# Issuing each Strassen product of an MLP together with its neighbour, one matmul of each in turn

## The chip, the cores and the metric

The kernel runs on 1 core of one Trainium2 chip. The metric is device time in microseconds (us) of one execution of the program. TensorE (PE) does the matmuls, and its weight loads are a row of their own (PEld); VectorE is DVE, ScalarE is ACT, GpSimd is POOL, SyncE is SP. Matmul results land in PSUM banks, all other tiles are in SBUF.

## What is computed

One layer of a hybrid encoder over 544 tokens (512 prompt, 32 sample), width 2048. The first part of the kernel (attention and mLSTM heads, output projection) is not touched. The change is in the MLP:

```python
x = x + jnp.concatenate([att, ml], axis=-1) @ p['w_out']
hn = rms_norm(x, p['norm2_w'])
x = x + jnp.square(jax.nn.relu(hn @ p['w_up'])) @ p['w_down']
```

`w_up` is 2048 x 8192 and `w_down` 8192 x 2048, all in float32. Every float32 operand is split into a high part in `fp32r` and a low part that holds the rest, and a product is the sum of three matmuls: high weights by high values, high weights by low values, low weights by high values.

## The kernel before

**Steps and products.** The MLP runs 64 steps: step 0 by 8 plain block products, steps 1 to 31 for the up projection (two tiles of 128 hidden columns each), steps 32 to 63 for the down projection. A step p from 1 on computes a 2 x 2 block result C11, C12, C21, C22 by seven products in place of eight (Strassen's scheme in Winograd's form). Product i (0 to 6) is a sum over 8 tiles k of 128, with three matmuls of 128 x 272 for each: 24 matmuls, all into one PSUM bank (`product`, L860). `Step(first, per, reg)` is a step number, inside a hardware loop one that counts with a register.

**The seven products' weights.** Each is a tile of 128 x 1024 in one of 4 slots (`SLOT`, L98): products 0 and 3 share slot 0, 1 and 4 slot 1, 2 and 6 slot 2, 5 has slot 3 alone. Weights are made in two passes. ACT copies the source to `wp_hi` (`wp_split`, L1200; I call it hi0 to hi6) when the product that used the slot before is done (`FREE_AFTER`, L100). Then DVE subtracts to get `wp_lo` (`wp_lo_part`, L1755; lo0 to lo6). The order on both is 0, 1, 5, 2, 3, 4, 6. The sources are blocks of the weight matrix loaded by SP (`wa`) or sums of them that DVE makes in `ws`: sum_1 (L1781), sum_2 (L1787), sum_3 (L1791), sum_4 (L1795). Product 3's weights come from sum_3, which stands on DVE directly behind lo2; hi3 (ACT) and lo3 (DVE) follow.

```python
SLOT = (0, 1, 2, 0, 1, 3, 2)
PLACE = (0, 1, 3, 4, 5, 2, 6)
FREE_AFTER = (-3, -2, 0, 1, 2, -1, 3)
```

**The results.** Three banks are used: y for products 0 and 4, x for 1, 3 and 5, z for 2 and 6. Products 4 and 6 accumulate on top of 0 and 2, and 3 and 5 go on top of what bank x holds. ACT copies product 0 out of its bank (`copy_y`, L1293), DVE combines the rest: `from_u` (L1872), `c22` (two instructions, L1876 and L1878), the copy of C11 (L1911 in an up step, L1998 in a down step), `c21` (L1882), `c12` (L1886).

**What follows in an up step.** DVE applies ReLU and the norm factor to C22, C21 and C12 (`relu`, L1890), ACT squares all four (L1288), and POOL makes the left-hand forms of the hidden tile with four subtractions and additions (`hidden_forms`, L567, L568, L570, L572) and stores them to memory. In a down step ACT and DVE turn a stored hidden tile into new entries of `forms_hi` and `forms_lo` (`refill`, L1348 and L1936, in three parts), and POOL adds C21/C22 and C11/C12 to the output in memory.

**Order.** Every engine works through a hand-written list, and semaphores tie the lists together: `product_done` counts finished products, `wp_hi_ready` and `wp_lo_ready` finished weights, `c11_done`, `c12_done`, `c21_done`, `c22_done`, `u_done`, `v_done` and `y_copied` results. A product waits for its own `wp_lo` and for its bank to be read. Between the up and the down steps, in step 32, the forms of the first 8 hidden tiles are loaded and converted (L430, L1277, L1767).

## Time and profile before

| | |
|---|---|
| runs | 2426.3, 2427.5, 2427.5 us; median 2427.5 |
| profiled execution | 2426.36 us, span of its records 2424.8 us |
| PE busy | 2400.3 us, 99% of the span, 18890 matmuls |
| DVE, ACT, POOL busy | 1776.0 (73%), 1084.8 (45%), 353.1 us (15%) |
| MLP steps 1 to 63 | from 1068.6 us to the last matmul's start at 2421.9 us, 10584 matmuls |
| mean granted TensorE clock | 0.998 of full speed |

The profile is one execution. A duration in it is that of one instruction from start to end; matmuls overlap, so a matmul of 0.29 us is followed by the next after some 0.126 us, and the distance of starts is what counts for PE. In the rows, "idle before" in brackets is how long the engine stood still ahead of an instruction, and what ended that.

### The profile page before, as it was taken

The page shows a single profiled execution, that of the slowest core. Times are in us where ns is not written, and L with a number is a line of the kernel's source. Part 1 is how long each engine was busy: PE and PEld are TensorE (multiplying, and loading weights), DVE is VectorE, ACT ScalarE, POOL GpSimd, SP SyncE. Part 2 cuts the span into 40 slices and gives each one's busy share as a digit, 9 for nine tenths or more (in the row PEclk, how much of TensorE's full clock was granted, in tenths as well). Part 3 has the DMA queues.
Part 4 walks back from the last instruction along what each step waited for, and adds up shares of the span by engine and source line. Part 5 has one row for each costly group of instructions (what it writes and reads, how often), then busy time and mean ns, then how long its engine had stood idle before and what let it go on. Part 6 is the DMA issues. An engine that isn't in the chain of part 4 may idle for free.

```text
span 2424.8 us, 48650 instructions
## 1 busy us (share of the span) xinstructions
PE 2400.3 (99%) x18890; PEld 2373.9 (98%) x18890; DVE 1776.0 (73%) x2568; ACT 1084.8 (45%) x1715; POOL 353.1 (15%) x408
## 2 busy tenths in 40 slices
PE   8999999999999999999999999999899999999999
PEld 8999999999999999989999999999899999999999
DVE  7466566665657664498888888888888888888887
ACT  5345353453534443364444444444544444444443
POOL 0000000000000100142222222222211101011110
PEclk9999999999999999999999999999999999999999
DMA  5423323333332524424434444444855555655554
GB/s 182 121 82 116 101 88 96 99 103 88 101 104 87 166 86 124 137 97 153 147 136 137 146 144 152 152 152 136 280 155 167 162 166 174 180 180 173 170 164 120
DMA packets 116109, 334.69 MB, mean 138 GB/s; under 512 B 13048, under 2 KB 20856, under 8 KB 116000
## 3 DMA queue, kind: packets, MB, share of 16 engines
q1 hardware_dynamic: 88352, 222.14, 28.0%
q0 software_dynamic: 26208, 106.60, 15.4%
q10 hardware_dynamic: 1440, 4.47, 0.5%
q8 instruction: 71, 1.16, 0.2%
q14 instruction: 38, 0.31, 0.0%
HBM read 274.07 MB, written 59.09 MB: 137 GB/s over the span
## 4 chain that ended last, share of the span: by engine, by line
PE 96%; DVE 2%; issue 1%; DMA 1%; ACT 0%; SPq 0%; DVEq 0%; ACTq 0%
PE psum L639 35%; PE psum L875 18%; PE psum L879 18%; PE psum L877 18%; DVE forms_lo L1767 1%; PE psum L795 1%; PE psum L664 1%; PE psum L721 1%; PE psum L735 1%; PE psum L764 1%; PE psum L679 0%; PE psum L697 0%; PE psum L695 0%; DMA form_raw<-hidden_forms 0%; PE psum L713 0%
## 5 line engine op out<-in xcount | busy, mean ns | idle before, releaser
L875 PE MATMUL psum<-forms_hi,wp_hi 128*128 128x272 f32 x3528 | 1024.6, 290 | 13.1 <-issue 8.9
L879 PE MATMUL psum<-forms_hi,wp_lo 128*128 128x272 f32 x3528 | 1022.5, 290 | 0.0
L877 PE MATMUL psum<-forms_lo,wp_hi 128*128 128x272 f32 x3528 | 1017.4, 288 | 0.0
L639 PE MATMUL psum<-act_tiles,w_hi 128*128 128x272 f32 x4544 | 758.5, 289 | 0.0
L875 PEld LDWEIGHTS psum<-forms_hi,wp_hi 128*128 128x128 f32 x3528 | 665.6, 189 | 14.6 <-issue 9.6
L877 PEld LDWEIGHTS psum<-forms_lo,wp_hi 128*128 128x128 f32 x3528 | 666.7, 189 | 0.0
L879 PEld LDWEIGHTS psum<-forms_hi,wp_lo 128*128 128x128 f32 x3528 | 665.4, 189 | 0.0
L639 PEld LDWEIGHTS psum<-act_tiles,w_hi 128*128 128x128 f32 x4544 | 642.7, 188 | 6.9 <-issue 4.0
L1200 ACT ACTIVATE wp_hi<-ws 128x1024 fp32r<-128x1024 f32 x252 | 267.3, 1061 | 625.3 <-DVE ws L1787 289.9
L639 PE MATMUL psum<-act_tiles,w_lo 128*128 128x272 f32 x2272 | 468.7, 288 | 0.0
L1755 DVE TENSOR_TENSOR wp_lo<-ws,wp_hi 128x1024 fp32r<-128x1024 f32 x252 | 309.6, 1229 | 89.0 <-ACT wp_hi L1200 87.7
L1390 DVE TENSOR_TENSOR w_lo<-w_raw,w_hi 128x512 fp32r<-128x512 f32 x288 | 200.1, 705 | 217.2 <-ACT w_hi L940 216.4
L639 PEld LDWEIGHTS psum<-act_tiles,w_lo 128*128 128x128 f32 x2272 | 355.6, 189 | 0.0
L940 ACT ACTIVATE w_hi<-w_raw 128x512 fp32r<-128x512 f32 x288 | 177.1, 627 | 318.4 <-PE psum L639 313.9
L1755 DVE TENSOR_TENSOR wp_lo<-wa,wp_hi 128x1024 fp32r<-128x1024 f32 x189 | 231.0, 1222 | 27.4 <-ACT wp_hi L1200 27.4
L1200 ACT ACTIVATE wp_hi<-wa 128x1024 fp32r<-128x1024 f32 x189 | 199.4, 1055 | 114.9 <-PE psum L879 110.6
L608 POOL DMA_DIRECT2D out_yT<-cbuf x62 | 52.2, 842 | 574.0 <-DVE cbuf L1882 499.8
L567 POOL TENSOR_TENSOR hid<-hid 128x272 f32<-128x272 f32 x32 | 37.4, 1170 | 480.7 <-ACT hid L1288 480.7
L1791 DVE TENSOR_TENSOR ws<-wa 128x1024 f32<-128x1024 f32 x63 | 94.5, 1500 | 0.0
L1781 DVE TENSOR_TENSOR ws<-wa 128x1024 f32<-128x1024 f32 x63 | 76.8, 1220 | 8.2 <-DMA wa<-in_wpairs 4.6
L1936 DVE TENSOR_TENSOR forms_lo<-hid,forms_hi 128x544 fp32r<-128x544 f32 (+1 forms) x93 | 75.7, 815 | 3.3 <-ACT forms_hi L1348 2.3
L1795 DVE TENSOR_TENSOR ws<-ws,wa 128x1024 f32<-128x1024 f32 x63 | 77.3, 1228 | 0.0
(319 smaller groups left out, 2105.8 us busy)
## 6 DMA issues: line engine op xcount, KB each, us to landing
wa<-in_wpairs SPq DMA_DIRECT2D x248, 512.0 KB, 4.4
w_raw<-in_wstream SPq DMA_DIRECT2D x291, 256.0 KB, 2.7
hidden_forms<-hid POOLq DMA_DIRECT2D x32, 952.0 KB, 4.2
hid<-hidden_forms POOLq DMA_DIRECT2D x31, 952.0 KB, 6.8
out_yT<-cbuf POOLq DMA_DIRECT2D x62, 272.0 KB, 4.6
form_raw<-hidden_forms SPq DMA_DIRECT2D x7, 1088.0 KB, 10.1
res<-in_xT POOLq DMA_DIRECT2D x16, 272.0 KB, 3.9
kc_sb<-in_kcT POOLq DMA_DIRECT2D x8, 512.0 KB, 4.3
```

Source lines behind the costliest of these rows:

```text
L639: last = nc.tensor.matmul(out[0:m, half, :], w[:, w_slot, col:col + m], x[:, half * HB:(half + 1) * HB], start=start and n_ == 0, stop=sto ...
L875: nc.tensor.matmul(bank, wp_hi[:, w, s], form_hi(i)[:, k, :], start=i < 3 and k == 0, stop=False, skip_group_check=True)
L877: nc.tensor.matmul(bank, wp_hi[:, w, s], form_lo(i)[:, k, :], start=False, stop=False, skip_group_check=True)
L879: last = nc.tensor.matmul(bank, wp_lo[:, w, s], form_hi(i)[:, k, :], start=False, stop=k == HALF - 1, skip_group_check=True)
L940: nc.scalar.activation(w_hi[:, slot, :], w_raw[:, slot, :], ACT.Copy).then_inc(hi_ready, 1)
L1200: nc.scalar.activation(wp_hi[:, SLOT[i], :], src, ACT.Copy).then_inc(wp_hi_ready, 1)
L1390: nc.vector.tensor_tensor(w_lo[:, slot, :], w_raw[:, slot, :], w_hi[:, slot, :].bitcast(f32), ALU.subtract).then_inc(lo_ready, 1)
L1755: nc.vector.tensor_tensor(wp_lo[:, SLOT[i], :], src, wp_hi[:, SLOT[i], :].bitcast(f32), ALU.subtract).then_inc(wp_lo_ready, 1)
L1781: nc.vector.tensor_tensor(ws[:, S_1, :], wa[:, A21, :], wa[:, A22, :], ALU.add).then_inc(s1_ready, 1)
L1791: nc.vector.tensor_tensor(ws[:, S_3, :], wa[:, A11, :], wa[:, A21, :], ALU.add).then_inc(s3_ready, 1)
L1795: nc.vector.tensor_tensor(ws[:, S_2, :], ws[:, S_2, :], wa[:, A12, :], ALU.add).then_inc(s4_ready, 1)
L1936: nc.vector.tensor_tensor(forms_lo[:, lo:lo + f.stop - f.start, s, :], hid[:, b, f, :], forms_hi[:, f, s, :].bitcast(f32), ALU.subtract).t ...
```

## The change

1. **Alternate issue.** A product is cut in two halves of 4 tiles k (12 matmuls). In the new `two_products` PE issues, one matmul of each in turn, the second half of product i and the first half of product i + 1 (of the next step's product 0 after product 6): 24 matmuls, which I call **phase i**. The waits of product i + 1 (`begin`) stand at the head of phase i. Steps 2 to 31 and steps 33 to 63 run so, 209 + 216 = 425 phases. The first half of each stretch's first product and the second half of its last are issued alone. Step 1 and step 32 keep whole products.
2. **Four banks.** Product 3 gets a bank of its own (bank 4), and products 3 and 5 start new sums in place of adding to bank x (`STARTS`).
3. **Output combinations.** `c22` becomes bank 4 plus `x_first`, then minus bank z; `c21` adds bank x to the first of these. The number of DVE instructions and their sizes in a steady step stay; some waits are added (`u_done`, `c22_done`).
4. **DVE order.** lo6 now stands ahead of c22, and sum_1 behind it (behind the first refill too in a down step). sum_3 and all of ACT's order, `SLOT` and `FREE_AFTER` stay.
5. **The last step** combines the old output with `x_first` and bank 4 in place of `y_first` and bank x.

```diff
+STARTS = (True, True, True, True, False, True, False)
...
-                def product(p, i, k_ready=None):
-                    bank = (bank_y, bank_x, bank_z, bank_x, bank_y, bank_x, bank_z)[i]
+                def begin(p, i):
                     pe.wait_ge(wp_lo_ready, (p * 7 + (PLACE[i] - 2)).v)
                     if i < 3:
                         pe.wait_ge((c11_done, c21_done, c12_done)[i], p.v)
                     elif i < 6:
-                        pe.wait_ge((u_done, y_copied, v_done)[i - 3], p.v)
+                        pe.wait_ge((c22_done, y_copied, u_done)[i - 3], p.v)
                     else:
                         pe.wait_ge(c22_done, (p + 1).v)
...
+                def two_products(p, i):
+                    after = (p, i + 1) if i < 6 else (p + 1, 0)
+                    begin(*after)
+                    for k in range(HALF // 2):
+                        for n_ in range(3):
+                            last = partial(i, k + HALF // 2, n_)
+                            if k == HALF // 2 - 1 and n_ == 2:
+                                last.then_inc(product_done, 1)
+                            partial(after[1], k, n_)
...
+                product(Step(2), 0, ks=early)
+                with pe.Fori(0, PAIRS - 3) as r:
                     for i in range(7):
-                        product(Step(2, 1, r), i)
+                        two_products(Step(2, 1, r), i)
+                for i in range(6):
+                    two_products(Step(PAIRS - 1), i)
+                product(Step(PAIRS - 1), 6, ks=late)
...
                 def c22(p):
+                    dve.wait_ge(u_done, p.v)
                     dve.wait_ge(product_done, (p * 7 + 4).v)
-                    nc.vector.tensor_tensor(cbuf[:, 1, 1, :], bank_x, y_first[:], ALU.subtract).then_inc(v_done, 1)
+                    nc.vector.tensor_tensor(cbuf[:, 1, 0, :], bank_4, x_first[:], ALU.add).then_inc(v_done, 1)
                     dve.wait_ge(v_done, p.v)
-                    nc.vector.tensor_tensor(cbuf[:, 1, 1, :], cbuf[:, 1, 1, :], bank_z, ALU.subtract).then_inc(c22_done, 1)
+                    nc.vector.tensor_tensor(cbuf[:, 1, 1, :], cbuf[:, 1, 0, :], bank_z, ALU.subtract).then_inc(c22_done, 1)
...
                     sum_4(p)
...
-                    sum_1(p + 1)
+                    wp_lo_part(p, 6)
                     dve.wait_ge(squared, (p * 4).v)
                     c22(p)
                     relu(p, cbuf[:, 1, 1, :], 1, c22_done)
-                    wp_lo_part(p, 6)
+                    sum_1(p + 1)
```

PE in the loop over the up steps, where product 3 begins. In a MATMUL row the tile that PE writes stands first, then the two it reads; a row's brackets hold what it waits for. Before, product 3's first matmul stands behind the whole of product 2:

```order
L879 MATMUL psum<-forms_hi,wp_lo 128x272
L864 REGISTER_ALU
L875 MATMUL psum<-forms_hi,wp_hi 128x272 [waits u_done,wp_lo_ready]
L877 MATMUL psum<-forms_lo,wp_hi 128x272
L879 MATMUL psum<-forms_hi,wp_lo 128x272
L875 MATMUL psum<-forms_hi,wp_hi 128x272
```

And with the change; the row with the wait is product 2's fifth tile (phase 2), and product 3's first matmul is the one behind it:

```order
L878 MATMUL psum<-forms_hi,wp_lo 128x272 x2
L864 REGISTER_ALU
L878 MATMUL psum<-forms_hi,wp_hi 128x272 [waits c22_done,wp_lo_ready]
L878 MATMUL psum<-forms_hi,wp_hi 128x272
L878 MATMUL psum<-forms_lo,wp_hi 128x272 x2
L878 MATMUL psum<-forms_hi,wp_lo 128x272 x2
```

The wait for product 3's weights now stands 12 matmuls earlier, and holds the second half of product 2 too.

DVE in the same loop, from product 6's end on, with the change (L1913 is c12, L1917 a ReLU, L1780 `wp_lo_part`: here lo2, then lo3 behind sum_3, L1816, then lo4 and lo6; L1897 is `from_u`, L1820 sum_4):

```order
L1913 TENSOR_TENSOR cbuf<-psum,x_first 128x272 [waits product_done]
L1917 SCALAR_TENSOR_TENSOR cbuf<-cbuf,rstd 128x272 [waits c12_done]
L1777 REGISTER_ALU
L1780 TENSOR_TENSOR wp_lo<-ws,wp_hi 128x1024 [waits wp_hi_ready]
L1816 TENSOR_TENSOR ws<-wa 128x1024 [waits wp_lo_ready]
L1777 REGISTER_ALU
L1780 TENSOR_TENSOR wp_lo<-ws,wp_hi 128x1024 [waits wp_hi_ready]
L1897 TENSOR_TENSOR x_first<-psum,y_first 128x272 [waits y_copied,product_done,c12_done]
L1777 REGISTER_ALU
L1780 TENSOR_TENSOR wp_lo<-wa,wp_hi 128x1024 [waits wp_hi_ready]
L1820 TENSOR_TENSOR ws<-ws,wa 128x1024 [waits wp_lo_ready]
L1777 REGISTER_ALU
```

And before, the same stretch (L1886 is c12, L1890 a ReLU, L1755 `wp_lo_part`, L1791 sum_3, L1872 `from_u`, L1795 sum_4):

```order
L1886 TENSOR_TENSOR cbuf<-psum,x_first 128x272 [waits product_done]
L1890 SCALAR_TENSOR_TENSOR cbuf<-cbuf,rstd 128x272 [waits c12_done]
L1752 REGISTER_ALU
L1755 TENSOR_TENSOR wp_lo<-ws,wp_hi 128x1024 [waits wp_hi_ready]
L1791 TENSOR_TENSOR ws<-wa 128x1024 [waits wp_lo_ready]
L1752 REGISTER_ALU
L1755 TENSOR_TENSOR wp_lo<-ws,wp_hi 128x1024 [waits wp_hi_ready]
L1872 TENSOR_TENSOR x_first<-psum,y_first 128x272 [waits y_copied,product_done,c12_done]
```

Nothing has moved between c12 and sum_4; the swap of lo6, c22 and sum_1 comes behind it.

## Rows read from the trace of the kernel before

**Rows 1.** The page: busy time of the engines.

```profile
PE 2400.3 (99%) x18890; PEld 2373.9 (98%) x18890; DVE 1776.0 (73%) x2568; ACT 1084.8 (45%) x1715; POOL 353.1 (15%) x408
```

**Rows 2.** What PE waited for from 1069 us on (total us, times, longest).

```profile
PE psum L875 <- issue: 8.9, 4, 5.0
PE psum L875 <- DVE wp_lo L1755: 4.3, 3, 2.2
```

**Rows 3.** L875 alone, 1500.2 to 1700: count, durations, first and last start.

```profile
L875 PE MATMUL psum<-forms_hi,wp_hi x528: 287/290/292, 1500.2 to 1699.6; 128*128 128x272 f32 x176
```

**Rows 4.** L639 alone, 938.4 to 1040.85, the output projection: same columns.

```profile
L639 PE MATMUL psum<-act_tiles,w_hi x544: 283/288/293, 938.4 to 1040.4; 128*128 128x272 f32 x182
L639 PE MATMUL psum<-act_tiles,w_lo x272: 282/288/291, 938.9 to 1040.7; 128*128 128x272 f32 x136
```

**Rows 5.** PE in step 0, two plain products by turns into two banks.

```profile
1057.32 0.41 PE L894 MATMUL psum<-forms_hi,wp_hi 128*128 128x272 f32 x2
...
1060.33 0.41 PE L894 MATMUL psum<-forms_hi,wp_hi 128*128 128x272 f32 x2
```

**Rows 6.** PE: last matmul of step 15's product 6, first of step 16's product 0.

```profile
1390.40 0.29 PE L879 MATMUL psum<-forms_hi,wp_lo 128*128 128x272 f32 x1
1390.53 0.29 PE L875 MATMUL psum<-forms_hi,wp_hi 128*128 128x272 f32 x1
```

**Rows 7.** ACT in up step 16: hi2, hi3.

```profile
1390.73 1.06 ACT L1200 ACTIVATE wp_hi<-ws 128x1024 fp32r<-128x1024 f32 x1 [0.58 <-PE psum L879]
...
1394.87 1.06 ACT L1200 ACTIVATE wp_hi<-ws 128x1024 fp32r<-128x1024 f32 x1 [2.44 <-DVE ws L1791]
```

**Rows 8.** DVE in up step 16: lo2, sum_3, lo3.

```profile
1391.82 1.22 DVE L1755 TENSOR_TENSOR wp_lo<-ws,wp_hi 128x1024 fp32r<-128x1024 f32 x1
1392.96 1.79 DVE L1791 TENSOR_TENSOR ws<-wa 128x1024 f32<-128x1024 f32 x1
1395.96 1.25 DVE L1755 TENSOR_TENSOR wp_lo<-ws,wp_hi 128x1024 fp32r<-128x1024 f32 x1 [1.21 <-ACT wp_hi L1200]
```

**Rows 9.** POOL in up steps 16 and 17: the first operation on each hidden tile.

```profile
1392.51 1.16 POOL L567 TENSOR_TENSOR hid<-hid 128x272 f32<-128x272 f32 x1 [14.59 <-ACT hid L1288]
...
1413.70 1.16 POOL L567 TENSOR_TENSOR hid<-hid 128x272 f32<-128x272 f32 x1 [14.62 <-ACT hid L1288]
```

**Rows 10.** DVE by groups: sum_3 in up steps (1100:1700), in down steps (1800:2370).

```profile
L1791 DVE TENSOR_TENSOR ws<-wa 128x1024 f32<-128x1024 f32 x28 | 50.1, 1790 | 0.0
L1791 DVE TENSOR_TENSOR ws<-wa 128x1024 f32<-128x1024 f32 x27 | 32.9, 1219 | 0.0
```

**Rows 11.** ACT, then DVE in down step 45: hi2; c12, lo2, sum_3, lo3.

```profile
2019.63 1.06 ACT L1200 ACTIVATE wp_hi<-ws 128x1024 fp32r<-128x1024 f32 x1 [0.68 <-PE psum L879]
...
2020.40 0.43 DVE L1886 TENSOR_TENSOR cbuf<-psum,x_first 128x272 f32<-128x272 f32 x1
2020.75 1.22 DVE L1755 TENSOR_TENSOR wp_lo<-ws,wp_hi 128x1024 fp32r<-128x1024 f32 x1
2021.89 1.22 DVE L1791 TENSOR_TENSOR ws<-wa 128x1024 f32<-128x1024 f32 x1
2024.31 1.23 DVE L1755 TENSOR_TENSOR wp_lo<-ws,wp_hi 128x1024 fp32r<-128x1024 f32 x1 [1.21 <-ACT wp_hi L1200]
```

**Rows 12.** DVE and PE where PE waited for weights, in step 1.

```profile
1071.01 1.22 DVE L1755 TENSOR_TENSOR wp_lo<-ws,wp_hi 128x1024 fp32r<-128x1024 f32 x1
...
1072.28 0.39 PE L875 MATMUL psum<-forms_hi,wp_hi 128*128 128x272 f32 x1 [0.47 <-DVE wp_lo L1755]
1072.51 0.29 PE L877 MATMUL psum<-forms_lo,wp_hi 128*128 128x272 f32 x1
```

**Rows 13.** Stretches: span, busy PE PEld DVE ACT POOL, granted clock, DMA share, GB/s.

```profile
1390.53:1411.72 21.19, 21.19 (x171) 21.19 (x170) 17.20 (x21) 8.88 (x12) 5.83 (x5) 1.00 0.43 145
1729.51:1765.19 35.68, 25.83 (x170) 25.01 (x169) 34.63 (x35) 22.64 (x28) 8.85 (x8) 0.86 0.79 274
2019.43:2040.62 21.19, 21.19 (x171) 21.19 (x169) 17.50 (x21) 9.48 (x11) 2.24 (x3) 1.00 0.58 172
```

More of the change, by code:

```diff
@@ L203, in build @@
         bank_y, bank_x, bank_z, bank_4 = (psum[:, i, 0:HB] for i in range(4))
+        BANKS = (bank_y, bank_x, bank_z, bank_4, bank_y, bank_x, bank_z)
         b11, b12, b21, b22 = (res[:, k, t] for k in (slice(HALF, KT), slice(0, HALF))
@@ L866, in product, with partial @@
                     elif i < 6:
-                        pe.wait_ge((u_done, y_copied, v_done)[i - 3], p.v)
+                        pe.wait_ge((c22_done, y_copied, u_done)[i - 3], p.v)
                     else:
                         pe.wait_ge(c22_done, (p + 1).v)
-                    for k in range(HALF):
+                    if p.first >= PAIRS + 1 and i in (0, 3, 5):
+                        pe.wait_ge(refill_lo, ((p + (-PAIRS)) * 3 + {0: -2, 3: -1, 5: 0}[i]).v)
+                def partial(i, k, n_):
+                    s, w = slice(k * P, (k + 1) * P), SLOT[i]
+                    weights, form = ((wp_hi, form_hi(i)), (wp_hi, form_lo(i)), (wp_lo, form_hi(i)))[n_]
+                    return nc.tensor.matmul(BANKS[i], weights[:, w, s], form[:, k, :], start=STARTS[i] and k == 0 and n_ == 0,
+                                            stop=k == HALF - 1 and n_ == 2, skip_group_check=True)
@@ L871, in product @@
+                def product(p, i, k_ready=None, ks=range(HALF)):
+                    if ks[0] == 0:
+                        begin(p, i)
+                    for k in ks:
                         if k_ready is not None and k % 4 == 0:
                             pe.wait_ge(form_lo_ready, k_ready + 1 + k // 4)
-                        s = slice(k * P, (k + 1) * P)
-                        w = SLOT[i]
-                        nc.tensor.matmul(bank, wp_hi[:, w, s], form_hi(i)[:, k, :], start=i < 3 and k == 0, stop=False,
-                                         skip_group_check=True)
@@ L877, in product @@
-                        nc.tensor.matmul(bank, wp_hi[:, w, s], form_lo(i)[:, k, :], start=False, stop=False,
-                                         skip_group_check=True)
-                        last = nc.tensor.matmul(bank, wp_lo[:, w, s], form_hi(i)[:, k, :], start=False,
-                                                stop=k == HALF - 1, skip_group_check=True)
-                    last.then_inc(product_done, 1)
+                        for n_ in range(3):
+                            last = partial(i, k, n_)
@@ new lines, in product @@
+                    if ks[-1] == HALF - 1:
+                        last.then_inc(product_done, 1)
[3 more added lines that the diff above has]
+                    for k in range(HALF // 2):
+                        for n_ in range(3):
+                            last = partial(i, k + HALF // 2, n_)
+                            if k == HALF // 2 - 1 and n_ == 2:
+                                last.then_inc(product_done, 1)
+                            partial(after[1], k, n_)
@@ L914, in _ @@
                     product(Step(1), i, 2 * FORM_AT[i])
+                early, late = range(HALF // 2), range(HALF // 2, HALF)
+                product(Step(2), 0, ks=early)
+                with pe.Fori(0, PAIRS - 3) as r:
+                    for i in range(7):
+                        two_products(Step(2, 1, r), i)
+                for i in range(6):
+                    two_products(Step(PAIRS - 1), i)
+                product(Step(PAIRS - 1), 6, ks=late)
+                for i in range(7):
+                    product(Step(PAIRS), i, 2 * (FORMS_UP + i))
+                product(Step(PAIRS + 1), 0, ks=early)
                 with pe.Fori(0, PAIRS - 2) as r:
                     for i in range(7):
[L917 to L928 removed]
+                        two_products(Step(PAIRS + 1, 1, r), i)
+                for i in range(6):
+                    two_products(Step(2 * PAIRS - 1), i)
+                product(Step(2 * PAIRS - 1), 6, ks=late)
             @block.scalar
@@ L1291, in copy_y @@
                     act.wait_ge(product_done, (p * 7 + 1).v)
-                    act.wait_ge(c21_done, p.v)
+                    if not (p.reg is None and p.first == 1):
+                        act.wait_ge(u_done, (p + (-1)).v)
                     nc.scalar.activation(y_first[:], bank_y, ACT.Copy).then_inc(y_copied, 1)
@@ L1986, in down @@
                         refill(t + (-1), 2)
-                    sum_1(p + 1)
-                    refill(t, 0)
+                    wp_lo_part(p, 6)
                     if first:
@@ L1993, in down @@
                     c22(p)
-                    wp_lo_part(p, 6)
+                    refill(t, 0)
+                    sum_1(p + 1)
                     if not first:
```

20 lines of the change are left out of this document (7 added, 13 removed).

## Prediction

> **What bounds the kernel now.** I read the page's busy times first: PE is busy 99% of the span [rows 1], so only two things can move the time: the distance between the starts of matmuls, and waits of PE that do not exist now. The list of PE's waits says how few there are: from the MLP's start at 1069 us on, 13.2 us in 7 waits [rows 2], all in steps 1 and 32. The stretches show it too: up step 16 and down step 45 last 21.19 us each, and PE is busy for all of it [rows 13].
>
> Next the distance of starts. A product is all in one bank. L875 is one matmul in three, and its 528 in steps 21 to 30 start from 1500.2 to 1699.6 [rows 3]: 199.4 us / (527 x 3) = **126.1 ns**. At the granted clock of 1.00 [rows 13], 2.4 GHz, 272 columns are 113 ns of streaming, so 13 ns are something else. The output projection has matmuls of the same size and writes two banks by turns. Its 816 run from 938.4 to 1040.7 [rows 4]: 102.3 / 815 = **125.5 ns**. In step 0 two products with different weights go by turns into two banks, and 24 matmuls take 1060.33 - 1057.32 = 3.01 us [rows 5], 125.4 ns.
>
> Last, the chain that makes weights, since every phase asks for its weights earlier. In step 16 product 6's last matmul of the step before starts at 1390.40 [rows 6]. hi2, which needs its slot, starts at 1390.73, then hi3 at 1394.87 [rows 7]; on DVE lo2, sum_3 and lo3 run from 1391.82, 1392.96 and 1395.96, the last until 1397.21 [rows 8]. Each waits for the one before: product 6, hi2 (ACT), lo2 (DVE), sum_3 (DVE), hi3 (ACT), lo3 (DVE). From hi2's start to lo3's end it is **6.48 us** in an up step. In down step 45 it is 2024.31 + 1.23 - 2019.63 = **5.91 us** [rows 11].
>
> **Part 1, the matmuls' distance.** The 425 phases hold 10,200 matmuls. They write two banks by turns, as in [rows 4, 5], and with different weights in turn, as in [rows 5]. I take 125.4 ns: 0.7 ns x 10,200 = **-7.1 us**. Bounds: nothing, if the 0.7 ns come from what else differs in those rows; 1.0 ns, if the rounded starts of [rows 5] hide 0.3, so -10.2 us.
>
> The Trainium skill (TensorE: Matmul & The Clock Gate, Back-to-back issue gap) gives N / 2.4 + 2.5 ns as the distance of warm matmuls, for 272 columns an estimate of 116 ns. No row here shows it, in one bank or in two; if alternating reached it, this term would be -105 us, taken alone.
>
> **Part 2, the wait for product 3's weights.** This decides. Before, product 0 frees slot 0 at its end, and product 3 starts two products later. Now product 3 starts at the head of phase 2, which is two phases behind product 6's end: 48 x 125.4 = 6.02 us after the end of phase 6. lo3 must be done by then, and its chain starts only with product 6's end. It used to have three products for it, 9.08 us.
>
> Up step: product 6's last matmul is now the last but one of its phase, so the phase ends 2 x 0.125 us after its start, and hi2 starts 0.33 - 0.25 = 0.08 us behind the phase's end (0.33 is 1390.73 - 1390.40, [rows 6, 7]). The chain adds 6.48: 6.56. Where PE waited for weights in step 1, the matmul started 0.05 us after lo's end at 1072.23, and the next followed after 0.23 instead of 0.126 us [rows 12]: 0.15 us more, 6.71. PE is ready at 6.02, so it stands **0.70 us**. This falls in steps 2 to 31, 30 times (in step 2 half a product more lies ahead of phase 2, but the chain is late there from step 1 as well): **+21.0 us**.
>
> Down step: 0.08 + 5.91 + 0.15 = 6.14, which is 0.12 us too late. Here lo2 starts at 2020.75, on the heels of c12 (2020.40), though hi2 was done at 2020.69 [rows 11]. DVE's own queue is as late as ACT, and PE's faster phases bring the demand some 0.03 us nearer; PE also has register instructions between its waits for the refill and the weights. I take **0.20 us**, 30 times (steps 34 to 63; step 33 has the half product ahead): **+6.0 us**. Bounds 0.05 and 0.35: +1.5 and +10.5 us.
>
> The up step's size hangs on sum_3. It takes 1.79 us in up steps and 1.22 in down steps [rows 10], and in up steps POOL's L567 runs from 1392.51 to 1393.67 across its start at 1392.96 [rows 8, 9]. POOL starts when the last square is made, which hangs on c12 and hi2, so on product 6's end as sum_3 does. Both keep their distance, and the 0.57 us stay. Bounds: 0 and 1.16 us (L567's whole length) in place of 0.57, which is 0.13 to 1.29 us of wait, +4 to +39 us; I stay at the row, since nothing moves one against the other.
>
> The Trainium skill (SBUF — State Buffer, Who interferes with whom) has DVE instructions with two SBUF inputs and POOL instructions that read SBUF lock each other out for a whole instruction. sum_3 would then wait for L567's end, 1393.67 - 1392.96 = 0.71 us, where the row shows 0.57; the sum with 0.71 is 4 us higher.
>
> **Part 3, the other waits, at nothing.** Product 4 needs lo4 one phase after product 1's end. hi and lo together last 2.34 us (hi3's start to lo3's end, [rows 7, 8]); with 0.08 and 0.15 that is 2.6 of 3.01 us. Product 2 needs lo2 one phase after product 6: 1391.82 + 1.22 - 1390.73 = 2.31, the same. Product 6 waits for c22: two DVE instructions behind product 3's end, within one phase, as lo6 now stands ahead and is made a phase earlier. If this cover went, each of them would cost what it is late by, 61 times. sum_1 moved back by some 3 us, and its wait and the loads of `wa` it reads have only more time; the copy of C11 behind it still waits for product 4's end. ACT's copy of bank y lies between hi3 and hi4 as before. DVE's busy time in a step stays 17.2 and 17.5 of 21.19 us [rows 13].
>
> **Part 4, the ends of the stretches.** Step 32 lasts 35.68 us with a granted clock of 0.86 [rows 13], because forms are loaded and converted; those loads wait for step 31's products. Each of these now ends half a product later against PE's total work, 1.5 us, and the last phases of step 31 bring PE there 0.7 us later by its own wait: **+0.8 us**. Bounds -1 and +6: a longer standstill can hold the clock at its lower level, 1.2 GHz, for longer. The end of the kernel hangs on product 6 of step 63 as before: nothing.
>
> **Sum.** -7.1 + 21.0 + 6.0 + 0.8 = +20.7 us on the profiled execution's 2426.4 us: **2447 us**. That execution lies 1.1 us below the median of the runs, less than I can resolve. A measurement of this kernel tells 0.2%, 4.9 us, from no change. A steady up step would last 6.02 + 0.70 + 5 x 3.01 = 21.8 us, a down step 21.3.
>
> **Rivals.**
>
> *Alternating gives nothing.* The distance stays at 126.1 ns. Then +7.1 is missing from the gain, less some 2 us, as phases 0 and 1 are longer by 0.03 us in all and the wait shorter by as much: 2452 us. For it: [rows 4] have other operands, too. Against it: [rows 5] have the MLP's own. 17%.
>
> *sum_3 is not slowed.* If POOL's work and sum_3 move apart, the up steps wait 0.13 us: 2447 - 17 = 2430 us, no change that can be told. Against it stands what I said of their common start. 8%.
>
> *The weights are in time.* The other side: the chain fits into two phases, PE never waits, and the gain of the first part is left: 2426.4 - 7.1 + 0.8 = 2420 us, faster. The place is the head of phase 2, and it decides at 6.02 - 0.15 - 0.08 = 5.79 us from hi2's start to lo3's end. The rows have 5.91 and 6.48, so DVE and ACT would have to be quicker by 0.1 and 0.7 us with unchanged instructions. 4%.
>
> *Matmuls much closer.* If writing one bank all the time is what costs most of the 13 ns, phases could shrink to 24 x 116 = 2.78 us. DVE's chain from product 4's end on then sets the step: in a down step 12.2 us to product 3's start (4 phases, 12.04 us, are what it has at 125.4 ns, with 0.2 over) and three phases, 20.6 us, in an up step 21.0. Against 21.19 that is -18 and -6 us: 2404 us. 116 ns is the figure of the page named above; from rows alone, -20.7 us is made good at 2.7 ns less on the 120 matmuls outside phases 0 and 1, 122.7 ns. Nothing in [rows 4, 5] is below 125.4. 4%.
>
> *The clock falls.* If a standstill of 0.7 us in every up step let the clock drop to 1.2 GHz for a time, a phase at that level would take 3.01 us more. For it: step 32's 0.86. Against it: there PE stood 9.9 us of 35.68 (busy 25.83, [rows 13]), and in steps of 21 us it would stand 3% of the time. Were it one phase in every second up step: 2447 + 15 x 3.01 = 2492 us. 3%.
>
> **How the numbers follow.** Forecast 62%, the rivals 17, 8, 4, 4 and 3%; 2% for something slower that I don't see. Faster by over 0.2%: the two rivals and a sliver, 9%. Within 0.2%: the unslowed sum_3, 8%. Slower: the rest, 83%. The range reaches from above the unslowed sum_3, 2433 (half the up steps' wait gone and 10.2 us gained), to 2460: no gain by alternating, 0.35 us in down steps and a worse step 32 (2452 + 4 + 4). Below it lie 13%, above it some 5%.
>
> **What would show it.** In the profile of the changed kernel: starts of matmuls inside a phase 125.4 ns apart; PE's waits led by `wp_lo`, some 60 times, at the head of phase 2 and nowhere else, about 0.6 us in up and 0.1 in down steps; step lengths of 21.8 and 21.3 us; sum_3 still 1.79 us in up steps. I am wrong if PE waits elsewhere, above all for lo2 or lo4; if sum_3 is back at 1.22 us there; or if the mean clock is below 0.99.

## The result and the profile after

The changed kernel takes **2449.1 us** (median of 4 runs, 2447.5 to 2449.9), the kernel before 2427.5 us (2426.3 to 2428.4). The ratio is 1.0088, with a 95% interval of 1.0071 to 1.0106: 21.6 us slower. The profiled execution has a span of 2447.4 us against 2424.8 us, 22.6 us more. The forecast was 2447 us, so the total is right; not all of its terms are.

The page of the changed kernel, busy times [rows 1]:

```profile
PE 2409.3 (98%) x18890; PEld 2370.3 (97%) x18890; DVE 1781.6 (73%) x2569; ACT 1084.7 (44%) x1715; POOL 353.7 (14%) x408
```

What PE waited for from 1069 us on, in total us, times and longest [rows 2]:

```profile
PE psum L878 <- DVE wp_lo L1780: 26.1, 38, 3.7
PE psum L878 <- DVE forms_lo L1792: 0.3, 1, 0.3
```

The same work (18890 matmuls), and 13 us of recorded waits have become 26 us, now nearly all for `wp_lo` (L1780 here). Short gaps are missing in this list: it counts 38 waits, while the starts of matmuls show 58 gaps at the head of phase 2 alone. So the distances of starts are what to read. Step 16, PE, the end of phase 6 with the first matmul of the step's phase 0 (x2: two matmuls in one row), then the last row of phase 1 and the head of phase 2:

```profile
1400.75 0.41 PE L878 MATMUL psum<-forms_hi,wp_lo 128*128 128x272 f32 x2
1401.00 0.42 PE L878 MATMUL psum<-forms_hi,wp_hi 128*128 128x272 f32 x2
...
1406.75 0.41 PE L878 MATMUL psum<-forms_hi,wp_lo 128*128 128x272 f32 x2
1407.63 0.52 PE L878 MATMUL psum<-forms_hi,wp_hi 128*128 128x272 f32 x2 [0.47 <-DVE wp_lo L1780]
1407.99 0.41 PE L878 MATMUL psum<-forms_lo,wp_hi 128*128 128x272 f32 x2
```

ACT, DVE and POOL in the same step: hi2, lo2, sum_3, hi3, lo3, and POOL's four operations on the hidden tile (L569 to L574) [rows 7 to 9]:

```profile
1401.08 1.06 ACT L1224 ACTIVATE wp_hi<-ws 128x1024 fp32r<-128x1024 f32 x1 [0.53 <-PE psum L878]
...
1402.17 1.23 DVE L1780 TENSOR_TENSOR wp_lo<-ws,wp_hi 128x1024 fp32r<-128x1024 f32 x1
1402.86 1.18 POOL L569 TENSOR_TENSOR hid<-hid 128x272 f32<-128x272 f32 x1 [15.14 <-ACT hid L1312]
1403.32 1.80 DVE L1816 TENSOR_TENSOR ws<-wa 128x1024 f32<-128x1024 f32 x1
...
1404.00 1.75 POOL L570 TENSOR_TENSOR hid<-hid 128x272 f32<-128x272 f32 x1
...
1405.23 1.06 ACT L1224 ACTIVATE wp_hi<-ws 128x1024 fp32r<-128x1024 f32 x1 [2.45 <-DVE ws L1816]
...
1405.71 0.79 POOL L572 TENSOR_TENSOR hid<-hid 128x272 f32<-128x272 f32 x1
...
1406.33 1.25 DVE L1780 TENSOR_TENSOR wp_lo<-ws,wp_hi 128x1024 fp32r<-128x1024 f32 x1 [1.21 <-ACT wp_hi L1224]
...
1406.58 1.64 POOL L574 TENSOR_TENSOR hid<-hid 128x272 f32<-128x272 f32 x1
```

The chain is the one of before, instruction for instruction. From hi2's start to lo3's end it takes 1407.58 - 1401.08 = 6.50 us (6.48 before). Phase 2, which holds product 3's first half, starts at 1407.63, 0.05 us behind lo3's end. The last matmul of phase 1 starts at 1406.88, so the gap is 0.75 us in place of 0.125, and the next distance 0.23 in place of 0.125: 0.63 + 0.10 = 0.73 us are lost. This stands in each of steps 3 to 31 (step 31 loses 0.05 us more), and nowhere else in them.

Step 45, a down step [rows 11]: hi2, c12 (L1913), lo2, sum_3, hi3, lo3, and ahead of c12 the conversion of the refill (L1963):

```profile
2042.50 1.06 ACT L1224 ACTIVATE wp_hi<-ws 128x1024 fp32r<-128x1024 f32 x1 [0.62 <-PE psum L878]
...
2042.69 0.72 DVE L1963 TENSOR_TENSOR forms_lo<-hid,forms_hi 128x544 fp32r<-128x544 f32 x1
...
2043.33 0.43 DVE L1913 TENSOR_TENSOR cbuf<-psum,x_first 128x272 f32<-128x272 f32 x1
...
2043.68 1.22 DVE L1780 TENSOR_TENSOR wp_lo<-ws,wp_hi 128x1024 fp32r<-128x1024 f32 x1
...
2044.81 1.22 DVE L1816 TENSOR_TENSOR ws<-wa 128x1024 f32<-128x1024 f32 x1
...
2046.14 1.06 ACT L1224 ACTIVATE wp_hi<-ws 128x1024 fp32r<-128x1024 f32 x1 [2.58 <-DVE ws L1816]
...
2047.23 1.23 DVE L1780 TENSOR_TENSOR wp_lo<-ws,wp_hi 128x1024 fp32r<-128x1024 f32 x1 [1.20 <-ACT wp_hi L1224]
```

lo3 is done at 2048.46, 5.96 us after hi2's start, and phase 2 starts at 2048.60: gap 0.30 us, with the slow next distance 0.28 us lost. Sixteen down steps look so. Twelve others lose 0.18 to 0.2 us, and one (step 38) loses 0.46. Step 63 has no gap and only the slow next distance, 0.10 us.

The stretches of step 16, of step 45 and of step 32 [rows 13]. Columns: span, busy PE, PEld, DVE, ACT, POOL, granted clock, DMA share, GB/s:

```profile
1748.91:1782.21 33.30, 26.32 (x168) 25.32 (x168) 33.20 (x33) 20.54 (x25) 7.96 (x7) 0.85 0.84 288
1401.00:1422.76 21.76, 21.29 (x170) 21.07 (x169) 17.32 (x21) 8.87 (x12) 5.84 (x5) 1.00 0.40 141
2042.42:2063.72 21.30, 21.28 (x170) 21.07 (x169) 17.52 (x21) 9.48 (x11) 2.23 (x3) 1.00 0.56 171
```

An up step lasts 21.76 us and a down step 21.30, in place of 21.19.

A place that the forecast left out is where alternation starts. PE in step 2: the last matmul of product 0's first half, which is issued alone, then phase 0:

```profile
1093.54 0.29 PE L878 MATMUL psum<-forms_hi,wp_lo 128*128 128x272 f32 x1
1095.62 0.51 PE L878 MATMUL psum<-forms_hi,wp_hi 128*128 128x272 f32 x2 [1.80 <-DVE wp_lo L1780]
```

PE stands 2 us for product 1's weights. DVE makes C11's copy, lo0, sum_2, and only then can hi1 and lo1 follow. Step 33 has the same gap (1783.70 to 1785.78). And behind both gaps the granted clock falls, 1.5 us after the gap's end in step 2 and 0.8 us in step 33. Two stretches of one length in step 2:

```profile
1095.62:1100.52 4.90, 4.89 (x27) 4.90 (x28) 4.64 (x5) 2.01 (x5) 2.44 (x2) 0.65 0.34 107
1100.52:1105.42 4.90, 4.90 (x41) 4.90 (x41) 2.67 (x3) 2.29 (x3) 3.36 (x4) 1.00 0.72 265
```

27 matmuls in 4.90 us and then 41. Some 15 of them are 0.227 us apart, at the lower level of 1.2 GHz: 1.5 us lost, twice.

**The account**, from the starts of the MLP's 10584 matmuls, after minus before, in us:

| place | us | forecast |
|---|---|---|
| 10,200 matmuls at 125.09 in place of 126.11 ns | -10.4 | -7.1 |
| head of phase 2, steps 3 to 31 (29 x 0.73) | +21.3 | +21.0 |
| head of phase 2, steps 34 to 62 (29 gaps, 7.1) and step 63 (0.1) | +7.2 | +6.0 |
| ahead of step 1, and step 1 itself (0.7 - 2.5) | -1.8 | 0 |
| start of alternation, steps 2 and 33 (2.0 + 2.1) | +4.1 | 0 |
| clock at 1.2 GHz behind these (2 x 1.5) | +3.0 | 0 |
| ahead of step 32 and step 32 itself (1.4 - 2.4) | -1.0 | +0.8 |
| sum | +22.4 | +20.7 |

The starts themselves end 22.6 us apart; 0.2 us stay unplaced.

### The profile page after: what moved, and what is told of

It is laid out like the page before. It is cut to its first block, busy times and chain, and to the rows that moved or that the text cites. A ratio compares the mean times of both kernels' runs of the same rounds, so it can differ in the third digit from the quotient of the medians.

```text
span 2447.4 us, 48692 instructions
## 1 busy us (share of the span) xinstructions
PE 2409.3 (98%) x18890; PEld 2370.3 (97%) x18890; DVE 1781.6 (73%) x2569; ACT 1084.7 (44%) x1715; POOL 353.7 (14%) x408
## 4 chain that ended last, share of the span: by engine, by line
PE 86%; DVE 8%; ACT 3%; issue 2%; DMA 1%; DVEq 0%; ACTq 0%; SPq 0%
PE psum L878 45%; PE psum L641 34%; ACT wp_hi L1224 3%; DVE wp_lo L1780 2%; DVE ws L1816 2%; DVE forms_lo L1792 1%; PE psum L797 1%; PE psum L666 1%; PE psum L723 1%; PE psum L737 1%; PE psum L766 1%; DMA form_raw<-hidden_forms 0%; PE psum L681 0%; PE psum L699 0%; PE psum L697 0%
## 5 line engine op out<-in xcount | busy, mean ns | idle before, releaser
L878 PE MATMUL psum<-forms_hi,wp_hi 128*128 128x272 f32 x3528 | 747.4, 290 | 26.7 <-DVE wp_lo L1780 26.1
L878 PE MATMUL psum<-forms_hi,wp_lo 128*128 128x272 f32 x3528 | 742.6, 289 | 0.0
L878 PE MATMUL psum<-forms_lo,wp_hi 128*128 128x272 f32 x3528 | 741.0, 288 | 0.0
L878 PEld LDWEIGHTS psum<-forms_hi,wp_hi 128*128 128x128 f32 x3528 | 559.3, 189 | 40.5 <-DVE wp_lo L1780 30.0
L878 PEld LDWEIGHTS psum<-forms_lo,wp_hi 128*128 128x128 f32 x3528 | 563.6, 189 | 0.0
L878 PEld LDWEIGHTS psum<-forms_hi,wp_lo 128*128 128x128 f32 x3528 | 557.8, 189 | 0.0
L1780 DVE TENSOR_TENSOR wp_lo<-ws,wp_hi 128x1024 fp32r<-128x1024 f32 x252 | 310.2, 1231 | 144.9 <-ACT wp_hi L1224 144.8
L1224 ACT ACTIVATE wp_hi<-wa 128x1024 fp32r<-128x1024 f32 x189 | 199.5, 1055 | 134.1 <-PE psum L878 129.6
L1780 DVE TENSOR_TENSOR wp_lo<-wa,wp_hi 128x1024 fp32r<-128x1024 f32 x189 | 230.7, 1221 | 27.0 <-ACT wp_hi L1224 27.0
L569 POOL TENSOR_TENSOR hid<-hid 128x272 f32<-128x272 f32 x32 | 37.8, 1182 | 499.8 <-ACT hid L1312 499.8
L1816 DVE TENSOR_TENSOR ws<-wa 128x1024 f32<-128x1024 f32 x63 | 94.9, 1506 | 0.0
L1820 DVE TENSOR_TENSOR ws<-ws,wa 128x1024 f32<-128x1024 f32 x63 | 77.4, 1228 | 0.0
L1812 DVE TENSOR_TENSOR ws<-wa,ws 128x1024 f32<-128x1024 f32 x63 | 76.8, 1220 | 0.0
```

What stands on the lines that cost most here:

```text
L569: nc.gpsimd.tensor_tensor(h[:, 2, :], h[:, 0, :], h[:, 7, :], ALU.subtract).then_inc(term_ready, 1)
L878: return nc.tensor.matmul(BANKS[i], weights[:, w, s], form[:, k, :], start=STARTS[i] and k == 0 and n_ == 0, stop=k == HALF - 1 and n_ == ...
L1224: nc.scalar.activation(wp_hi[:, SLOT[i], :], src, ACT.Copy).then_inc(wp_hi_ready, 1)
L1780: nc.vector.tensor_tensor(wp_lo[:, SLOT[i], :], src, wp_hi[:, SLOT[i], :].bitcast(f32), ALU.subtract).then_inc(wp_lo_ready, 1)
L1812: nc.vector.tensor_tensor(ws[:, S_2, :], wa[:, A11, :], ws[:, S_1, :], ALU.add).then_inc(s2_ready, 1)
L1816: nc.vector.tensor_tensor(ws[:, S_3, :], wa[:, A11, :], wa[:, A21, :], ALU.add).then_inc(s3_ready, 1)
```

## The experiments

Twelve kernels, in three batches. In their diffs "-" is the kernel that each starts from. For the distance of matmuls I give the mean of all starts inside products or phases (about 10,000 in each kernel, without gaps over 0.14 us), and where it decides the row of a group of matmuls from 1500 to 1700 us, from which it can be had to 0.1 ns as in [rows 3].

### Is it sum_3 on the chain? sum3_early and pool_after_sum3

sum3_early, from the changed kernel: sum_3 is made a product earlier, directly behind sum_2, and what stood ahead of lo2 and can wait goes behind it. The diff is of an up step; in a down step sum_3 moves likewise, and `refill(t, 1)` goes behind lo2.

```diff
+                    sum_3(p + 1)
...
-                    relu(p, cbuf[:, 1, 0, :], 0, c21_done)
...
-                    relu(p, cbuf[:, 0, 1, :], 1, c12_done)
                     wp_lo_part(p + 1, 2)
-                    sum_3(p + 1)
+                    relu(p, cbuf[:, 1, 0, :], 0, c21_done)
...
+                    relu(p, cbuf[:, 0, 1, :], 1, c12_done)
```

> The changed kernel with sum_3 of the next step taken on DVE directly behind sum_2 instead of behind lo2; the ReLU of C21 moves behind c12, in down steps the second refill behind lo2, so that lo2 keeps its place. My theory: PE's waits at the head of phase 2 come from the chain product 6, hi2, lo2, sum_3, hi3, lo3. With sum_3 out of it, hi3 needs only product 0's end, and lo3 is done some 0.5 us before PE asks. All waits of 0.63 us (up) and 0.2 us (down) go, the distance of matmuls stays at 125.1 ns: about 2449 - 22 - 8 = 2419 us, faster than before by 0.3%. Rival: two phases are too short for ACT and DVE in any order, and the wait only moves, to lo2 at phase 1 or to c22 at phase 5: 2435 us or more, with waits at another product. PE's list of waits tells them apart.

Measured: **2420.4 us** (2419.8 to 2421.0), ratio 0.9972 (0.9962 to 0.9983). Its up steps last 21.03 to 21.08 us, its down steps 21.00. PE's waits from 1069 us on:

```profile
PE psum L878 <- DVE wp_lo L1780: 12.3, 8, 2.3
PE psum L878 <- DVE forms_lo L1792: 0.3, 1, 0.3
```

DVE by groups, 1100 to 1700 (us in total, mean ns; L1816 is sum_3, L1780 the `wp_lo` made from `ws`):

```profile
L1780 DVE TENSOR_TENSOR wp_lo<-ws,wp_hi 128x1024 fp32r<-128x1024 f32 x114 | 151.8, 1332 | 78.7 <-ACT wp_hi L1224 78.7
L1816 DVE TENSOR_TENSOR ws<-wa 128x1024 f32<-128x1024 f32 x28 | 34.2, 1220 | 0.0
```

The steady waits are gone, but for 0.05 us in an up step (in the changed kernel L1780 means 1233 and L1816 1801 ns there). POOL now meets lo3, which takes 1.61 us in step 16 and is still done 0.12 us before phase 2 starts. The gaps of steps 2 and 33 stay, at 2.35 us. So the order of a few DVE instructions decides the sign of this change.

pool_after_sum3 keeps the changed kernel's DVE order, and holds POOL back instead:

```diff
+                    pool.wait_ge(s3_ready, (p + 1).v)
                     nc.gpsimd.tensor_tensor(...)
```

> The changed kernel with POOL's work on a hidden tile waiting for sum_3 as well. My theory: 0.57 us of the up steps' wait is sum_3 being slowed by POOL's subtraction across its start. sum_3 then takes 1.22 us in up steps, PE's wait there falls from 0.63 to about 0.1 us: 2449 - 17 = 2432 us; down steps stay. Rival: POOL's work now meets lo3 instead, which becomes longer by about as much: sum_3 at 1.22, lo3 at 1.8 us, time within 5 us of 2449. Second rival: POOL has nothing to do with it, sum_3 stays at 1.79.

Measured: **2436.7 us** (2436.3 to 2437.5), ratio 1.0040 (1.0025 to 1.0055). Between the two. DVE and POOL in step 16: sum_3, lo3 (L1781 here), and POOL's two operations beside it:

```profile
1397.95 1.22 DVE L1817 TENSOR_TENSOR ws<-wa 128x1024 f32<-128x1024 f32 x1
1399.26 0.77 POOL L570 TENSOR_TENSOR hid<-hid 128x272 f32<-128x272 f32 x1 [16.09 <-DVE ws L1817]
...
1399.99 0.77 POOL L571 TENSOR_TENSOR hid<-hid 128x272 f32<-128x272 f32 x1
...
1400.38 1.46 DVE L1781 TENSOR_TENSOR wp_lo<-ws,wp_hi 128x1024 fp32r<-128x1024 f32 x1 [1.21 <-ACT wp_hi L1225]
...
1400.72 1.76 POOL L573 TENSOR_TENSOR hid<-hid 128x272 f32<-128x272 f32 x1
```

sum_3 is back at 1.22 us, so POOL was what stretched it: shown. But the next link, lo3, takes 1.46 us in place of 1.25, since POOL now meets that one. Of the 21 us lost at the head of phase 2 in the up steps 11 are left, where my expectation, 17 us off the total, would have left 4. Its first rival, POOL meeting lo3, came true in part: the collision moved along the chain instead of leaving it.

The rows of both kernels say how much such a meeting costs. In the table, the overlap is the time from an instruction's start to the end of the other engine's instruction that was under way; unhindered, the DVE instructions take 1.22 us and POOL's 0.77.

| instruction, and what was under way at its start | overlap, us | longer by |
|---|---|---|
| sum_3 behind POOL's L569 | 0.72 | 0.58 |
| POOL's L569 behind lo2 | 0.54 | 0.41 |
| POOL's L570 behind sum_3 | 1.12 | 0.98 |
| POOL's L574 behind lo3 | 1.00 | 0.87 |
| lo3 behind POOL's L572 | 0.17 | 0.03 |
| pool_after_sum3: lo3 behind POOL's L571 | 0.38 | 0.24 |
| pool_after_sum3: POOL's L573 behind lo3 | 1.12 | 0.99 |

Each is longer by its overlap less 0.13 or 0.14 us: whichever started second waited for the end of the first. The steps from 1120 to 1700 us show the same throughout.

### What do the other parts do? whole_products

From the changed kernel: four banks, regrouped combinations and DVE order stay, and each product is issued whole.

```diff
-                        two_products(Step(2, 1, r), i)
+                        product(Step(2, 1, r), i)
```

> The changed kernel with whole products issued one after another as before; four banks, the new output combinations and the new order on DVE stay. My theory: these parts cost and bring nothing; the distance of matmuls is 126.1 ns, PE has no waits in steady steps (two whole products lie between product 6 and product 3), 21.19 us a step: 2427.5 us, within 3 us. Rival: the output combinations or the order bring or cost something of their own, then it differs by more than that.

Measured: 2424.4 us (2423.7 to 2425.5), ratio 0.9990 (0.9981 to 1.0000): just under the kernel before, by less than 0.2%. I had expected 2427.5 within 3 us, so it lies at that edge. The distance is 126.11 ns and no steady step waits. Its 2 us against before lie at the ends of the stretches: step 1 gains 2.5 us and step 2 gives 1.7 back, step 32 gains 2.6 and step 33 gives 1.1 back. Which of the three parts gives these 2 us was not tested. As they cost nothing together, the loss of the changed kernel is all in the alternate issue.

### What brings the matmuls closer? Eight kernels

My forecast put the smaller distance down to two banks used by turns. **two_banks_before**, from the kernel before, sends every second matmul to bank 7, which nobody reads, so half of each sum is left out:

```diff
+                            odd = (3 * k + n_ + 1) % 2
-                        nc.tensor.matmul(bank, ...)
+                            last = nc.tensor.matmul(psum[:, 7, 0:HB] if odd else bank, ...)
```

> The kernel before, whole products one after another, but in steps 1 to 63 every second matmul writes another bank that nobody reads, so half of each product's sum is left out. Tells whether the bank or the mixing of products brings matmuls closer. If the bank does it, as I hold: the distance falls from 126.1 to 125.1 ns, a steady step lasts 168 x 125.1 = 21.02 us, and the kernel about 2427 - 10 = 2417 us. If it is that weights and values of two products come by turns: 126.1 ns and 2427 us.

Measured: 2426.5 us in its one run, so the expectation missed. Its matmuls of one kind, 1500 to 1700 us:

```profile
L877 PE MATMUL psum<-forms_hi,wp_lo x530: 287/289/291, 1499.8 to 1699.9; 128*128 128x272 f32 x177
```

200.1 us / (529 x 3) = 126.1 ns, as before. **one_bank_alternating** is the counterpart, from the changed kernel; only a product's last matmul goes to its own bank, and the sums are left out of the output:

```diff
-                    return nc.tensor.matmul(BANKS[i], ...)
+                    end = k == HALF - 1 and n_ == 2
+                    return nc.tensor.matmul(BANKS[i] if end else psum[:, 7, 0:HB], ...)
```

> The changed kernel with its alternating order, waits and semaphores, but all matmuls of an MLP product except the last of each write bank 7; only a product's last goes to its own bank (so the sums are left out of the output). Theory A, mixing: the smaller distance of starts inside a phase comes from the weights and values of two products in turn, not from two banks. Then the distance stays at 125.1 ns and the time near 2449 us. Theory B, banks (my prediction's): in one bank the distance is back at 126.1 ns, and the time is 2449 + 10.5, less some 2 us of shorter standstills, near 2457 us. I expect A, 125.1 ns.

Measured: 2449.1 us in its one run, 125.08 ns inside phases, and 21.3 us lost at the head of phase 2 in the up steps, as in the changed kernel. Both agree: **the bank has no part in it**. What is left is the order in which the matmuls read their operands.

The next idea: weights or values that follow each other twice cost 3.3 ns. **k_pairs_before**, from the kernel before, puts another tile's matmul between:

```diff
-                    for k in range(HALF):
+                    order = [(k + h, n_) for k in range(HALF // 2) for n_ in range(3) for h in (0, HALF // 2)]
+                    for j, (k, n_) in enumerate(order):
```

> The kernel before, whole products as they are, but within a product tiles k and k + 4 are issued one matmul of each in turn (the product with the stepwise wait in the first steps keeps its order). Same bank, no wait moved. Theory A, in its simplest form: what costs the 1 ns is that the same weights, or the same values, follow each other back to back; with another tile's between them the distance falls to 125.1 ns, and the time by 10.3 us to about 2417 us, 0.9957 of the kernel before. Rival: two different products are needed (their tiles lie in different slots), then 126.1 ns and 2427 us, ratio 1.000. I expect 2417 us, with little certainty.

Measured: **2416.6 us** (2415.2 to 2417.1), ratio 0.9956 (0.9943 to 0.9970). Here two of six matmuls are of this kind, first of a pair to second of a pair:

```profile
L879 PE MATMUL psum<-forms_lo,wp_hi x534: 284/287/291, 1499.8 to 1699.4; 128*128 128x272 f32 x178
```

From the first of a pair to the second of the last pair: 199.6 us / (266 x 6 + 1) = **125.0 ns**. The whole gain of alternating is there inside one product, with no weights wanted earlier. The expected time was met by luck: it came from the idea of repeats, which the next kernels refute.

The remaining kernels change the same line only; `order` lists the pairs of tile k and matmul (0 high by high, 1 high by low, 2 low by high):

```diff
+order = [(k, n_) for k in range(HALF) for n_ in (0, 2, 1)]                                     # values_twice_before
+order = [(k, n_) for k in range(HALF) for n_ in (2, 0, 1)]                                     # two_repeats_before
+order = [(k + h, n_) for k in range(0, HALF, 2) for n_ in range(3) for h in (0, 1)]            # neighbour_tiles_before
+order = [(k + h, n_) for k in range(HALF // 2) for h in (0, HALF // 2) for n_ in range(3)]     # tile_jumps_before
```

no_repeats_before issues matmul 0 of each tile one tile later: 1 and 2 of tile k, then 0 of tile k - 1.

> The kernel before, with the three matmuls of a tile in the order high weights by high values, low weights by high values, high weights by low values: now the values repeat back to back, and the weights do not. If the 1 ns comes from weights that repeat (one repeat in three before, none here), the distance falls to 125.1 ns, about 2417 us. If it comes from values that repeat (none inside a tile before, one here), it rises, to some 127 ns, about 2437 us. If repeats do not matter, it stays at 126.1 ns and 2427 us. I expect the first.

Measured: 2427.4 us in its one run, 126.11 ns. My expectation missed; the repeats had only changed from weights to values, so the idea could still stand. The last batch was to count repeats.

> The kernel before, with each tile's order low weights by high values, high by high, high by low: two of three matmuls repeat something of the one ahead (first the values, then the weights). Theory A, repeats at 3.3 ns each: 125.00 + 2 x 1.11 = 127.2 ns, 10,500 matmuls by 1.1 ns more, about 2439 us, 1.0047. Theory C, distance of tiles: the order of tiles is unchanged, so 126.1 ns and 2427 us. I expect A.

Measured: 2427.4 us (2426.5 to 2428.1), ratio 1.0002 (0.9992 to 1.0011), 126.11 ns. Missed.

> The kernel before, one product at a time, tiles in order, but each tile's high-by-high matmul is issued one tile later (high by low and low by high of tile k, then high by high of tile k - 1). No matmul shares weights or values with the one ahead of it. Theory A, repeats: a matmul that has its weights or its values in common with the one ahead costs 3.3 ns (the 1.11 ns by which 126.11 exceeds 125.00, on one of three matmuls). Then 125.0 ns and about 2416 us, 0.9957. Theory C, tiles: what counts is how far apart in SBUF the tiles of neighbours lie (4 tiles in the kernel that pairs k and k + 4), not repeats; then it stays near 126.1 ns, 2427 us. I expect A.

Measured: 2421.5 us (2421.0 to 2422.6), ratio 0.9978 (0.9969 to 0.9988), 125.56 ns: neither theory's number. One in three of its matmuls:

```profile
L879 PE MATMUL psum<-forms_hi,wp_hi x532: 285/288/289, 1499.8 to 1699.8; 128*128 128x272 f32 x178
```

> The kernel before, with tiles k and k + 1 (k even) issued one matmul of each in turn: no repeat, and the tiles lie next to each other in SBUF. Theory A, repeats: 125.0 ns, about 2416 us. Theory C, distance of tiles: near 126.1 ns, about 2427 us. I expect A.

Measured: 2419.1 us in its one run, 125.28 ns; missed by little, but the difference is real in the records (pairs again, 200.1 / 1597 = 125.3):

```profile
L879 PE MATMUL psum<-forms_hi,wp_hi x534: 286/288/290, 1499.8 to 1699.9; 128*128 128x272 f32 x178
```

> The kernel before, with whole tiles (three matmuls each, one repeat in three as before) in the order 0, 4, 1, 5, 2, 6, 3, 7. Theory A, repeats: 126.1 ns and 2427 us. Theory C, distance of tiles: the distance falls for the matmul at each change of tile, between 125.0 and 125.8 ns, 2416 to 2424 us. I expect A.

Measured: **2416.4 us** in its one run, 125.00 ns (199.9 us / (533 x 3) = 125.0):

```profile
L879 PE MATMUL psum<-forms_lo,wp_hi x534: 287/288/296, 1499.8 to 1699.7; 128*128 128x272 f32 x178
```

I had expected 2427 us. This fells the theory of repeats: whole tiles, one repeat in three as before, and the full gain. Together, by what a product's 24 matmuls take over 24 x 125.00 ns:

| order of tiles | repeats in 3 | ns | over, per product |
|---|---|---|---|
| 0 1 2 ... (before, two_banks, values_twice) | 1 | 126.11 | 26.7 |
| 0 1 2 ..., two_repeats | 2 | 126.11 | 26.7 |
| 1 1 0 2 2 1 ..., no_repeats | 0 | 125.56 | 13.3 |
| 0 1 0 1 0 1 2 3 ..., neighbour_tiles | 0 | 125.28 | 6.7 |
| 0 4 0 4 0 4 1 5 ..., k_pairs | 0 | 125.00 | 0 |
| 0 0 0 4 4 4 1 1 1 ..., tile_jumps | 1 | 125.00 | 0 |

What counts is **the order in which a product's tiles are read**. Orders that take tiles 4 apart together have no surplus; the plain order has 26.7 ns a product, 3.3 ns for each of its 8 tiles. The changed kernel pairs tile k + 4 of one product with tile k of the next, which is 4 apart too, and this fits its 125.09 ns.

Why the order counts is not settled. A tile is 512 bytes of weights and 1088 bytes of values in a partition, so its addresses are one suspect, but no run moved the tiles themselves. And the surplus can't be put down to single changes of tile. Over 53 steady steps the mean distance ahead of each of a product's first six matmuls is 122.5, 120.9, 134.1, 125.0, 121.7 and 124.2 ns in k_pairs_before, and the same to 0.1 ns in tile_jumps_before and in phase 0 of the changed kernel, although the first changes tile at every matmul and the second at every third. In the kernel before it is 126.7, 127.5, 127.5, 126.7, 130.0 and 120.0 ns, and the same in values_twice_before. Only the sum over a product is shown to follow the order.

### The version that comes out: k_pairs_regrouped

whole_products with k_pairs' order inside each product:

```diff
+                        for k in range(HALF // 2):
+                            for n_ in range(3):
+                                partial(i, k, n_)
+                                last = partial(i, k + HALF // 2, n_)
```

> The changed kernel's four banks, output combinations and DVE order with whole products (which took 2424.4 us, distance 126.1 ns), and within each product tiles k and k + 4 one matmul of each in turn. If repeats of the same weights or values are the cause of the 1 ns: 2424.4 - 10.3 = 2414 us, 0.9948 of the kernel before, with no steady wait for product 3's weights. If two different products are needed: 2424 us, ratio 0.999.

Measured: **2413.3 us** (2412.6 to 2413.5), ratio 0.9943 (0.9930 to 0.9957), the fastest of all. The expected 2414 us was taken from the idea of repeats, so here too the number was right and its reason wrong. PE's waits from 1069 us on, and a stretch that lasts as long as one up step:

```profile
PE psum L878 <- DVE wp_lo L1775: 9.4, 8, 2.2
PE psum L878 <- DVE forms_lo L1787: 0.3, 1, 0.3
```

```profile
1400.00:1421.00 21.00, 21.00 (x171) 21.00 (x170) 17.31 (x21) 8.87 (x13) 5.82 (x5) 1.00 0.43 147
```

Steps of 21.00 us, with PE busy throughout.

## Why the prediction was right, and where not

**What bounds the kernel, and the failing link: right.** The wait named (product 3's weights, at the head of phase 2), its chain and its size held: 0.73 us against 0.70 in up steps, with a chain of 6.50 us against 6.48. It falls 29 times, not 30. sum3_early takes one link out and with it the loss.

**sum_3 and POOL: right.** They kept their distance (1404.04 - 1403.32 = 0.72 us of overlap, 1.80 us for sum_3), so the 0.57 us stayed. pool_after_sum3 and sum3_early both bring 1.22 us back. That POOL's work would find the next link as well stood in the expectation of the former only as a rival. On the Trainium skill (SBUF — State Buffer, Who interferes with whom), whose rule is that the two share one port pair as an exclusive lock ("for the whole instruction" it says only of DVE's 2-port modes): the trace agrees for these instructions with two SBUF inputs, since the second always waited for the end of the first, less 0.13 to 0.14 us. The 0.57 us of the rows were an overlap of 0.71 less that.

**Part 1: right in sign, wrong in cause and size.** The step that failed is "They write two banks by turns", taken as the reason for 125.4 ns. Banks do nothing (two_banks_before, one_bank_alternating); the order of tiles does. The term was mis-sized by 3.3 us: -10.4 in place of -7.1, just past its bound of -10.2. The rows it was taken from differ in their order of tiles as well, so that the sign came out right was luck in part. The estimate came from [rows 4, 5], other orders of tiles; the bound from the rounding of [rows 5] was the better guess. No kernel came near 116 ns, the estimate from the Trainium skill (TensorE: Matmul & The Clock Gate, Back-to-back issue gap), whose formula that section gives for single matmuls and not for a stream with a weight load each, as here: the least mean over a product was 125.00 ns, 11.7 ns over 272 columns at one a cycle of 2.4 GHz.

**Part 2, down steps: right, 1.2 us short.** 7.2 in place of 6.0. In a step like 45 it is 0.08 + 5.96 + 0.14 + 0.10 - 6.00 = 0.28 us. The row names DVE's queue, as guessed: the refill's conversion runs from 2042.69 and c12 follows it, so lo2 starts 1.18 us after hi2 in place of 1.12; PE's start is 0.14 us behind lo3 in place of 0.05.

**Part 2, step 2, and Part 3: wrong for the first step of each stretch.** "The other waits, at nothing" took the steady step for all. Where alternation starts, product 1's weights are wanted half a product after product 0 begins, and DVE has C11's copy, lo0 and sum_2 ahead of lo1: 2.0 and 2.1 us. Step 2 then has no wait in phase 2.

**Part 4: right only in sum.** Step 32 is shorter by 2.4 us, which whole_products gives as well, and PE stands 1.4 us ahead of it, for product 0's weights, which DVE makes behind the first conversions of forms (lo0 ends at 1748.86, step 32 starts at 1748.91). The forecast had one term, for the loads of the forms, and neither of these.

**The rival of a falling clock: right in kind, small.** The gaps of 0.7 us in each up step left the granted clock at 1.00. The 2 us gaps at the start of alternation did not: 3.0 us in two places. The rival's price was too high as well: it doubled the distance, 3.01 us more for a phase, where matmuls at 1.2 GHz were 0.227 us apart, 2.4 us more for 24 of them.

The unforeseen terms are +4.1, +3.0, -1.8 and -1.0, +4.3 us in all where Part 4 had +0.8. Together they exceed Part 4's term by 3.5 us, and Part 1's miss of 3.3 us cancels that; the down steps' 1.2 us are most of what is left. So the total is 2 us off partly by luck, and the terms are not that good.

**The odds of the range.** The forecast puts 13% below 2433 us, but its own odds for the outcomes that lie there, faster (9%) and unchanged (8%), make 17%.

## What to carry to other kernels

Before two units of work are interleaved (issued by turns, one instruction of each), list what each needs at its start: to mix two halves is to ask for the second one's inputs half a unit earlier, and here 29 waits of 0.7 us outweighed 10 us of gain. Ask then whether the gain needs two units at all; here a reordering inside one product gave the same distance and moved no deadline. And read the first and last steps of a loop that is newly pipelined by themselves, as their waits are not those of the steady step.
